# Inverse roots of three recurrent heads by Newton steps on VectorE, in place of a root on ScalarE and a reciprocal

## The reference, cut to what matters

```
h = num / jnp.maximum(jnp.abs(den), jnp.exp(-m_comb))[..., None]
...
h_ml = rmsnorm(h_ml, ml_head_norm.reshape(ML_HEADS, ML_V))
h_ml = h_ml * jax.nn.sigmoid(o_ml.astype(jnp.float32)).reshape(B, S, ML_HEADS, ML_V)
```

## Time and profile before

| | |
|---|---|
| median of three runs | 1511.37 us (1510.83 to 1511.81) |
| the profiled execution | 1513.8 us, span 1512.0 us |
| TensorE (PE) busy | 1491.3 us, 99% |
| VectorE (DVE) busy | 1128.0 us, 75% |
| ScalarE (ACT) busy | 751.4 us, 50% |
| GpSimd (POOL) busy | 626.8 us, 41% |

### The profile page before, as it was taken

The page is one execution under the profiler, slowest core; times in us unless marked ns, Lnnn a source line. Parts: engine busy times, 40 slices in busy tenths (PEclk is TensorE's granted clock), DMA queues, the critical chain, the costliest instruction groups (busy, mean ns, idle before and its releaser), DMA issues.

```text
span 1512.0 us, 20174 instructions
## 1 busy us (share of the span) xinstructions
PE 1491.3 (99%) x6978; PEld 1231.2 (81%) x6978; DVE 1128.0 (75%) x1872; ACT 751.4 (50%) x1255; POOL 626.8 (41%) x280
## 2 busy tenths in 40 slices
PE   9999999999999999999999999999999999999998
PEld 7888888878888887888888888787778888888887
DVE  5689999997865445776776768788755887777776
ACT  6554333455562345754544345464963745444434
POOL 3455444332334432144444445451534344444451
PEclk9999999999999999999999999999999999999999
DMA  5343233345443323333333123233643432333551
GB/s 212 98 124 99 95 94 95 92 157 157 157 157 98 98 83 112 104 93 97 112 98 109 52 85 97 84 98 93 186 140 105 142 117 90 109 122 114 142 136 56
DMA packets 77026, 170.40 MB, mean 113 GB/s; under 512 B 22660, under 2 KB 39172, under 8 KB 76680
## 3 DMA queue, kind: packets, MB, share of 16 engines
q1 hardware_dynamic: 75920, 165.64, 35.2%
q10 hardware_dynamic: 1016, 3.61, 0.7%
HBM read 154.54 MB, written 14.69 MB: 112 GB/s over the span
## 4 chain that ended last, share of the span: by engine, by line
PE 87%; ACT 4%; DVE 4%; issue 3%; POOL 1%; DMA 1%; SPq 0%; DVEq 0%; ACTq 0%; POOLq 0%
PE bank L795 86%; DMA w_raw<-in_stream 1%; POOL w_lo L655 1%; ACT w_hi L1604 1%; DVE x_sq L2359 0%; ACT l_probs L2129 0%; DVE bias L2441 0%; ACT l_probs L2135 0%; ACT dn_first L1898 0%; POOL res L764 0%; DMA dn_raw<-in_stream 0%; PE bank L1214 0%; DVE res_tok L3421 0%; PE bank L905 0%; ACT ml_square L2080 0%
## 5 line engine op out<-in xcount | busy, mean ns | idle before, releaser
L655 POOL TENSOR_TENSOR w_lo<-w_raw,w_hi 128x1024 fp32r<-128x1024 f32 x191 | 473.2, 2487 | 518.1 <-ACT w_hi L1604 510.4
L795 PE MATMUL bank<-a_hi,w_hi 128*128 128x512 f32 (+1 forms) x1120 | 444.8, 397 | 2.2 <-DVE a_lo L3284 1.8
L795 PE MATMUL bank<-a_hi,w_lo 128*128 128x512 f32 (+1 forms) x1120 | 431.4, 385 | 0.0
L795 PE MATMUL bank<-a_lo,w_hi 128*128 128x512 f32 (+1 forms) x1120 | 431.2, 385 | 0.0
L1604 ACT CAST w_hi<-w_raw 128x1024 fp32r<-128x1024 f32 x199 | 204.6, 1046 | 174.9 <-DMA w_raw<-in_stream 174.5
L795 PEld LDWEIGHTS bank<-a_hi,w_hi 128*128 128x128 f32 x1120 | 210.5, 188 | 49.0 <-issue 4.2
L795 PEld LDWEIGHTS bank<-a_lo,w_hi 128*128 128x128 f32 x1120 | 210.6, 188 | 45.2 <-issue 3.4
L795 PEld LDWEIGHTS bank<-a_hi,w_lo 128*128 128x128 f32 x1120 | 210.4, 188 | 42.6
L667 POOL TENSOR_TENSOR dn_rest<-dn_raw,dn_second 128x1024 fp32r<-128x1024 f32 x39 | 93.7, 2431 | 248.3 <-DVE dn_rest L2734 248.3
L795 PE MATMUL bank<-dn_rest,f_hi 128*128 128x512 f32 x364 | 141.7, 389 | 0.0
L1898 ACT CAST dn_first<-dn_raw 128x1024 fp32r<-128x1024 f32 x54 | 55.6, 1047 | 157.9 <-DVE dn_raw L2715 157.9
(11 more groups left out here) (428 smaller groups left out, 2763.5 us busy)
## 6 DMA issues: line engine op xcount, KB each, us to landing
w_raw<-in_stream SPq DMA_DIRECT2D x199, 512.0 KB, 3.5
dn_raw<-in_stream SPq DMA_DIRECT2D x56, 512.0 KB, 3.6
p_parts<-d_parts SPq DMA_DIRECT2D x8, 640.0 KB, 3.9
d_turned<-p_parts SPq DMA_DIRECT2D x32, 160.0 KB, 3.3
l_turned<-p_parts SPq DMA_DIRECT2D x32, 160.0 KB, 3.1
p_parts<-l_parts SPq DMA_DIRECT2D x8, 384.0 KB, 3.3
res<-in_xT ACTq DMA_DIRECT2D x1, 2048.0 KB, 9.1
p_parts<-l_parts SPq DMA_DIRECT2D x8, 256.0 KB, 2.4
```

The costliest lines, as they stand in the source:

```text
L655: nc.gpsimd.tensor_tensor(w_lo[:, j, :], w_raw[:, j, :], w_hi[:, j, :].bitcast(F32), ALU.subtract).then_inc(w_lo_done, 1)
L795: return nc.tensor.matmul(o, l, r, start=start, stop=stop)
```

## The change

For heads 0, 1 and 2 the root and the reciprocal are replaced by `inverse_root` on VectorE: a start value from the number's bits (`ROOT_SEED`), and three Newton steps. It is issued at `st` 8, behind the diagonals of the next head (the loop of `ml_rest` is turned round for that). Each instruction waits for the one before it (`chained`). The variance, a product and a second copy of the estimate lie in columns 496 to 511 of bank 1, which nothing else uses (`norm_work`), so that each instruction of the Newton steps has at most one operand in SBUF. Head 3 keeps ScalarE's root and the reciprocal.

```diff
+        norm_work = ps[1][:, 256 + 2 * P - 4 * TB:].rearrange("p (i t) -> p i t", t=TB)
...
-                if st == 8:
+                if st == 8 and h == ML_HEADS - 1:
                     act.wait_ge(sems["ml_var"], h + 1)
-                    A.activation(mcol[:, 3, :], mcol[:, 2, :], ACT.Sqrt).then_inc(sems["ml_root"], 1)
+                    A.activation(mcol[:, 3, :], norm_work[:, 2, :], ACT.Sqrt).then_inc(sems["ml_root"], 1)
...
-                    V.scalar_tensor_tensor(out=mcol[:, 1, :], in0=mcol[:, 0, :], scalar=EPS, in1=mcol[:, 0, :],
+                    V.scalar_tensor_tensor(out=norm_work[:, 1, :], in0=mcol[:, 0, :], scalar=EPS, in1=mcol[:, 0, :],
...
+            def inverse_root(h):
+                square, y = mcol[:, 0, :], mcol[:, 3, :]
+                part, x, y_bank = norm_work[:, 0, :], norm_work[:, 2, :], norm_work[:, 3, :]
+                dve.wait_ge(sems["ml_var"], h + 1)
+                for copy in (y, y_bank):
+                    chained(V.tensor_scalar(copy.bitcast(I32), x.bitcast(I32), -0.5, ROOT_SEED, ALU.mult, ALU.add))
+                for i in range(ROOT_STEPS):
+                    chained(V.scalar_tensor_tensor(out=square, in0=y_bank, scalar=-0.5, in1=y,
+                                                   op0=ALU.mult, op1=ALU.mult))
+                    chained(V.tensor_tensor(part, square, x, ALU.mult))
+                    if i < ROOT_STEPS - 1:
+                        chained(V.scalar_tensor_tensor(out=y_bank, in0=part, scalar=1.5, in1=y,
+                                                       op0=ALU.add, op1=ALU.mult))
+                        chained(V.scalar_tensor_tensor(out=y, in0=part, scalar=1.5, in1=y,
+                                                       op0=ALU.add, op1=ALU.mult))
+                V.scalar_tensor_tensor(out=y, in0=part, scalar=1.5, in1=y, op0=ALU.add, op1=ALU.mult
+                                       ).then_inc(sems["ml_inv"], 1)
...
+                if st == 8 and h < ML_HEADS - 1:
+                    inverse_root(h)
                 if st == 9:
-                    dve.wait_ge(sems["ml_root"], h + 1)
-                    V.reciprocal(mcol[:, 3, :], mcol[:, 3, :]).then_inc(sems["ml_inv"], 1)
+                    if h == ML_HEADS - 1:
+                        dve.wait_ge(sems["ml_root"], 1)
+                        V.reciprocal(mcol[:, 3, :], mcol[:, 3, :]).then_inc(sems["ml_inv"], 1)
...
-                for h in range(ML_HEADS):
+                for h in reversed(range(ML_HEADS)):
                     ml_step(h, n - ML_START - ML_EVERY * h)
```

More of the change, by code:

```diff
@@ L222 @@
 GATES_AT = 1
+ROOT_SEED = float(0x5F3759DF)
+ROOT_STEPS = 3
 LATE_CASTS = 17
@@ L2078, in ml_step @@
                     act.wait_ge(sems["ml_out"], 4 * (h + 1))
+                    if h >= 1:
+                        act.wait_ge(sems["ml_var"], h)
                     for qb in range(TB):
@@ L3106, in ml_score_step @@
                         dve.wait_ge(sems["ml_floor"], 4 * h + 2 * i + 2)
-                    V.scalar_tensor_tensor(out=mcol[:, 1, :], in0=mcol[:, 0, :], scalar=EPS, in1=mcol[:, 0, :],
+                    V.scalar_tensor_tensor(out=norm_work[:, 1, :], in0=mcol[:, 0, :], scalar=EPS, in1=mcol[:, 0, :],
                                            op0=ALU.mult, op1=ALU.mult).then_inc(sems["ml_den"], 1)
                     dve.wait_ge(sems["ml_den"], h + 1)
-                    V.scalar_tensor_tensor(out=mcol[:, 2, :], in0=mcol[:, 2, :], scalar=1.0 / ML_V,
-                                           in1=mcol[:, 1, :], op0=ALU.mult, op1=ALU.add).then_inc(sems["ml_var"], 1)
+                    V.scalar_tensor_tensor(out=norm_work[:, 2, :], in0=mcol[:, 2, :], scalar=1.0 / ML_V,
+                                           in1=norm_work[:, 1, :], op0=ALU.mult, op1=ALU.add).then_inc(sems["ml_var"], 1)
+            def inverse_root(h):
[15 more added lines that the diff above has]
+                                       ).then_inc(sems["ml_inv"], 1)
             def ml_step(h, st):
```

## The result

| | before | changed |
|---|---|---|
| median | 1511.37 us (5 runs, 1510.81 to 1514.01) | 1516.52 us (5 runs, 1516.26 to 1520.06) |
| profiled execution, span | 1513.8, 1512.0 us | 1516.27, 1514.5 us |
| PE / DVE / ACT / POOL busy | 1491.3 / 1128.0 / 751.4 / 626.8 us | 1493.1 / 1135.2 / 743.7 / 626.6 us |

The ratio is 1.0036, 95% interval [1.0024, 1.0047]: the medians differ by 5.2 us, and the interval doesn't reach no change. The forecast was 1517.4 us (1512.8 to 1520.0).

A forecast was written before the change was run, and what follows sets the result against it. TensorE, busy 99% of the span, was taken as the bound. Head delays of +1.8, +0.9 and +1.6 (+4.3 us) and a clock drop of +1.7 gave +6.0 on the 1511.4 us median: 1517.4 us, range 1512.8 to 1520.0.

The forecast's parts named there:

- the mechanism and its place: VectorE's 13 added instructions delay ml_rows and sT, pausing TensorE; ScalarE's relief gives back at most 2.1 us.
- the price of a step: VectorE's 13 dependent instructions: 0.20 us each from start to start, 2.5 us a head, ends 1.7 and 3.3.
- the three heads: TensorE's added delay at heads 0, 1 and 2: +1.8, +0.9 and +1.6 us, sum +4.3, ends 1.9 and 6.7.
- the clock: TensorE's clock: one further drop, most likely at head 1, +1.7 us; the drop at head 2 stays.
- the placement: The 13 behind the diagonals: keeps GpSimd's start and ScalarE's decay from waiting for them, but not the rest.
- Rival 3: ScalarE's relief wins: pauses before sT at heads 1 and 2 and the clock drop go; -4.7, 1506.7 us; chance 0.11.
- Rival 1: Same delays at the three heads, no further clock drop: +4.3, 1515.7 us; chance 0.27.
- Rival 2: Two further clock drops, or steps of 0.26 us: +7.7 or +8.4, about 1519.5 us; chance 0.12.

The follow-up runs named there:

- E3: The changed kernel with one Newton step in place of three, 5 small instructions a head in place of 13: 1511.04 us, ratio 0.9992 to the kernel before.
- E5: The changed kernel with Newton steps for heads 1 and 2 alone, head 0 back on ScalarE's Sqrt and VectorE's reciprocal: 1514.81 us, ratio 1.0022.
- E10: The changed kernel itself, unchanged, measured a second time beside the kernel before: 1519.22 us, ratio 1.0049.
- E6: The changed kernel with the loop of ml_rest in its old direction, the 13 instructions ahead of the next head's diagonals: 1518.27 us, ratio 1.0040.
- E1: The kernel before with ScalarE's Sqrt replaced by Square for heads 0, 1 and 2, needing no table load: 1510.71 us, ratio 0.9988.
- E11: The kernel before itself, unchanged, measured again as the measure of no change: 1512.34 us, ratio 1.0003.
- E8: The changed kernel with two Newton steps, 7 small instructions a head, laid between VectorE's other work: 1512.05 us, ratio 1.0000 to the kernel before.
- E2: The changed kernel plus an unread ScalarE Sqrt with its two table loads for heads 0, 1 and 2: 1521.93 us, ratio 1.0055 to the kernel before.
- E7: The changed kernel with norm_work in 16 free columns of SBUF in place of bank 1: 1526.69 us, ratio 1.0098 to the kernel before.

## Why the prediction was right

**Right: the mechanism and its place.** VectorE's 1.41 us of waiting for ScalarE in front of `sT` vanished at head 1, TensorE pauses at the places named, and ScalarE's time turned into waiting for `rowinv`. The pauses in front of the second score blocks were forecast as 1.5, 0.9 and 1.2 us and came as 1.06, 0.48 and 0.94; the one in front of head 1's transposes as 1.4 and came as 1.82.

**Right: the price of a step.** 0.20 us from start to start, in the bank or not, 2.45 us a head; E3 shows that time follows the count. An instruction that writes to the bank took 0.166 to 0.172 us, one that writes to SBUF 0.161.

**Mis-sized: the three heads.** Forecast +1.8, +0.9, +1.6; measured +1.34, +1.22, +0.69; 3.25 instead of 4.3. The idle marks of VectorE's rows are too short to add up; the times from one start to the next hold more.
- Head 0: before, `sT` started 0.23 us behind the small accumulator read in front of it (1068.03 to 1068.26), in the changed kernel at the same time as it (both 1069.59). These 0.23 us have no idle mark in the earlier trace rows and were not counted; VectorE was 2.0 us late at `sT`, not 2.3. The wait for the transposes was 0.66 us counted so, not 0.53.
- Head 1: the norm itself began later. VectorE stood 0.37 us for `ml_square` and 0.16 for `mix_hi`, since ScalarE's own queue had been pushed back. E5, with head 0 back on ScalarE, has neither wait, and its pause for `ml_rows` is 0.70 us shorter. The forecast had ScalarE in time everywhere, and each head's delay to itself.
- Head 2: the L3107 that GpSimd held for 0.31 us too long in the earlier trace rows was not held this time (0.17 us), and about 0.4 us more of VectorE's idle time before, in front of the latent mask, `mix_lo` and `sT`, went than the 0.5 + 0.2 of the forecast. This head varies from execution to execution: 1.33 in E10, for the transfer shown there.

**Wrong in the reckoning: the clock.** The forecast added one drop, most likely at head 1, and kept the one at head 2. It then added the sum to the median of the kernel before. But that median is of executions without the drop at head 2 (1511.4 against 1513.0 with it), while the profile had it. In the first measurement the median execution is of the kind whose profile has no drop at head 1: its 5.2 us are 3.2 of delay, and the other 2 fit the one drop behind head 2, which by the mean clocks 35 of the 82 executions before have, and all ten of the changed kernel. The drop at head 1 comes in some, as E10's profile shows it; together with the longer low clock behind head 2 it gives 1519 to 1521 us.

So it was partly luck that 1517.4 came so near to 1516.5. Three things offset each other: delays 1.1 us too large, a drop at head 1 that the median execution didn't have, and a drop at head 2 that was missing from the distance. With the second measurement's 1519.2 the forecast is 1.8 us too low.

**Hardly needed: the placement.** I said that it keeps GpSimd's start and ScalarE's decay. Without it GpSimd starts 2.5 us later at head 1 (E6), but TensorE never waits for that, and ScalarE's decay is behind the mask in either order. What it did keep off, in one profile, are the 0.65 us at head 2, which nobody had foreseen.

**Rivals.** Rival 3, ScalarE's relief on top, is bounded by E1: 1.8 us and not 4.7. Even with nothing on VectorE's queue it would not have reached its 1506.7. Its sum also takes 0.48 us of pause that TensorE didn't have, and a clock drop that executions of 1511.4 us don't have by their mean clock. Rival 1, the delays without a drop at head 1, is what the first profile shows, with 3.25 us in place of 4.3; its 1515.7 is as near to the first median as the forecast is. Rival 2's clock, a drop more at two places, is nearest to E10's profile, and its 1519.5 to the second median. Ten executions don't decide among the three.

**Open.** What decides in one execution whether the clock drops. The total of the pauses doesn't: E5's profiled execution paused for 3.0 us at head 2 and kept its clock; the kernel before paused for 2.0 there, in both of its profiles, and lost it. The traces hold a hint. The first record of the full clock comes between 4.25 and 7.42 us from the start of the span, differently in each execution. In the four profiles whose first drop is behind head 2 (before, E11, changed, E8) the drop comes 1105.9 us after that record (in the kernel before 1110.51 after 4.59); in the four with a drop at head 1 (E10, E2, E6, E7) it comes 1085.4 us after it. So the moment of a drop goes with how the execution began, and the same pauses can fall well or badly against it. No run moved the one against the other, and filling TensorE's pauses with other work to see the drop go was not tried.

## What to carry to other kernels

Moving work from a full engine to another pays only where the first is what is waited for, and costs its full chain wherever the second stands in front of the bounding engine's next instruction: here 13 dependent instructions of 0.16 us cost 2.5 us of queue. A chain of small dependent instructions costs its latency (0.20 us each) when it stands alone and about 0.07 to 0.10 when each has an independent one behind it, so lay it between other work before changing anything else. Count idle time from start to start, since the marks leave some out, and don't take a wait of a weight load for a pause of TensorE. Before adding a sum to a median, look whether the profiled execution is of the same kind as the median one, by the mean clock that each run lists.

## What the runs showed of the hardware that was not expected

- A `TENSOR_SCALAR` of 128 x 4 int32 with one SBUF input was held by GpSimd for 2.35 us in E7 just as those with two inputs were; the instruction just before it, with the same input, ended as GpSimd started (1085.37 and 1085.38) and took 0.15. The Trainium skill ("GPSIMD Engine Reference", section "Specifications") names instructions in a two-port mode beside those with two SBUF inputs; that is in line with it, but the rows don't show the mode.
- A held instruction waits for one of GpSimd's instructions, and the next of the chain is caught by the next: three in a row, 5.8 us. So a chain of small instructions can be held once for each of them.
- Pauses have a second price. The low clock behind them cost 1.7 us (the mean of 0.66 over 5 us in the changed kernel's profile), more than any of the three heads' delays.
- The small instruction L3113, which squares a value from SBUF and writes to the bank, still has both inputs in SBUF in the changed kernel, and was held for 0.82 us in E6. Putting the output into the bank doesn't protect it.
